# A two-block model on one core: x and c loaded first, eight products on GpSimd, and another order of attention steps and modulation pieces

## What is computed

```python
mod = c @ ada_w[l] + ada_b[l]                       # 6 x 1024 numbers: shifts, scales, gates
sh1, sc1, gt1, sh2, sc2, gt2 = split(mod, 6)
h = rmsnorm(x, norm1_g[l]) * (1.0 + sc1) + sh1
xr, yr, q, k, v, ga, gb = split(h @ w_in[l], 7)     # w_in: 1024 x 7168
xr = causal_dwconv(xr, conv_w[l], conv_b[l])
y_a = rg_lru(xr, ...) * gelu(yr)                    # a linear recurrence over the positions
q, k = head_rmsnorm(q, q_norm_g[l]), head_rmsnorm(k, k_norm_g[l])
y_b = stick_breaking_attention(q, k, v)             # 8 heads of 128
mix = sigmoid(ga) * y_a + sigmoid(gb) * y_b
x = x + gt1 * (mix @ w_out[l])
h2 = rmsnorm(x, norm2_g[l]) * (1.0 + sc2) + sh2
up = causal_dwconv(h2 @ ffn_up[l], ffn_conv_w[l], ffn_conv_b[l])
x = x + gt2 * ((gelu(up[:half]) * up[half:]) @ ffn_down[l])
```

## Time and profile before

| What | us |
|---|---|
| median of 3 runs | 1760.31 |
| lowest and highest | 1758.86 and 1767.95 |
| the profiled execution's own time | 1761.02 |
| its span | 1759.2 |
| TensorE busy | 1606.3 (91%) |
| VectorE busy | 620.0 (35%) |
| ScalarE busy | 351.0 (20%) |
| GpSimd busy | 0.2 (0%) |
| DMA, mean over the span | 310 GB/s |

### The profile page before, as it was taken

The page is one execution under the profiler, slowest core; times in us unless marked ns, Lnnn a source line. Parts: engine busy times, 40 slices in busy tenths (PEclk is TensorE's granted clock), DMA queues, the critical chain, the costliest instruction groups (busy, mean ns, idle before and its releaser), DMA issues. The chain is left out here.

```text
span 1759.2 us, 20527 instructions
## 1 busy us (share of the span) xinstructions
PE 1606.3 (91%) x7254; PEld 887.2 (50%) x7254; DVE 620.0 (35%) x1429; ACT 351.0 (20%) x647; POOL 0.2 (0%) x4
## 2 busy tenths in 40 slices
PE   1999899999999897879999988899999999999894
PEld 1888788788888674733333322233333333333222
DVE  5547762589720367232121111111112111221111
ACT  1124563332210124131111111101111111111102
POOL 0000000000000000000000000000000000000000
PEclk8999899999999998879999999999999999999998
DMA  9836673457863330229999999999999999999993
GB/s 399 343 126 245 266 284 132 153 224 295 366 255 127 124 131 1 96 86 380 416 416 416 415 417 416 417 416 417 416 417 400 383 383 416 416 417 415 417 415 127
DMA packets 93604, 545.46 MB, mean 310 GB/s; under 512 B 8944, under 2 KB 9456, under 8 KB 44304
## 3 DMA queue, kind: packets, MB, share of 16 engines
q1 hardware_dynamic: 92144, 540.74, 76.5%
q10 hardware_dynamic: 1312, 2.75, 0.4%
HBM read 542.41 MB, written 1.05 MB: 309 GB/s over the span
## 5 line engine op out<-in xcount | busy, mean ns | idle before, releaser
L898 PE MATMUL bank<-ring,scr 128*64 128x512 f32 x2048 | 456.5, 598 | 19.4 <-DMA ring<-in_w_mlp 19.2
L501 PE MATMUL bank<-hT,ring 128*128 128x256 f32 x1856 | 415.8, 385 | 24.5 <-ACT hT L1070 24.0
L501 PEld LDWEIGHTS bank<-hT,ring 128*128 128x128 f32 x1856 | 358.6, 194 | 79.6 <-issue 28.8
L898 PEld LDWEIGHTS bank<-ring,scr 128*64 128x64 f32 x2048 | 142.9, 137 | 314.5 <-issue 255.5
L931 PE MATMUL bank<-ring,hT 128*64 128x512 f32 x1024 | 234.1, 597 | 4.6 <-DMA ring<-in_w_mlp 3.5
L2090 DVE TENSOR_SCALAR scr<-bank 128x256 f32<-128x256 f32 x64 | 27.0, 422 | 396.4 <-PE bank L898 396.4
L931 PEld LDWEIGHTS bank<-ring,hT 128*64 128x64 f32 x1024 | 68.5, 136 | 143.6 <-issue 131.4
L2156 DVE COPY hT<-bank 64x512 f32<-64x512 f32 x32 | 22.2, 695 | 320.1 <-PE bank L931 290.2
L1359 ACT ACTIVATE scr<-scr 128x256 f32<-128x256 f32 x64 | 26.7, 417 | 503.8 <-DVE scr L2090 503.8
L1463 DVE SCALAR_TENSOR_TENSOR ring<-ring,cb 128x1024 f32<-128x1024 f32 x96 | 113.3, 1220 | 9.8 <-DMA cb<-in_cb 6.3
L646 PE MATMUL bank<-scr,ring 128*128 128x256 f32 x384 | 83.5, 379 | 1.6 <-ACT scr L1215 1.6
(11 more groups left out here) (365 smaller groups left out, 1288.4 us busy)
## 6 DMA issues: line engine op xcount, KB each, us to landing
ring<-in_w_mlp SPq DMA_DIRECT2D x384, 1024.0 KB, 20.1
ring<-in_w_in SPq DMA_DIRECT2D x28, 1024.0 KB, 20.4
ring<-in_ada_w SPq DMA_DIRECT2D x24, 1024.0 KB, 8.4
ring<-in_up SPq DMA_DIRECT2D x24, 1024.0 KB, 5.7
ring<-in_w_ada SPq DMA_DIRECT2D x24, 1024.0 KB, 7.5
ring<-in_down SPq DMA_DIRECT2D x12, 1024.0 KB, 13.9
ring<-in_w2in SPq DMA_DIRECT2D x6, 1024.0 KB, 9.5
ring<-in_w_out SPq DMA_DIRECT2D x4, 1024.0 KB, 8.0
```

The costliest lines, as they stand in the source:

```text
L501: ins = mm(b[:, 256 * j:256 * j + 256], v[:, k * 256 + j * 128:k * 256 + j * 128 + 128], rhs[:, k, :], start=(k == 0), stop=(k == 7))
L898: ins = mm(HID[0][n][64 * hf:64 * hf + 64, :], K.xe[0][x % 2][:, xo:xo + 64], v[:, o0:o0 + 512], start=False, stop=(k == 7), skip_group_ch ...
```

## The change

- `lay_pieces`: the modulation pieces (1, k) come two for each c instead of three pieces for each c; the pieces (2, 0) to (2, 4) lie between the ga chunks and (2, 5) to (2, 7) between the gb chunks.
- Start: SyncE issues `xT` and `cb` ahead of all ring pieces, ScalarE only `con` and then `col`. ScalarE loads the root's table at once, squares x and takes the root before it looks at `lam`. VectorE takes the reciprocal behind two modulation pieces instead of four; the eight products are made by GpSimd, in a new function `gpsimd_program`.
- Attention: step 7 moves behind the first ga chunk; steps 8, 9, 10 follow the next three; steps 11 and 12 the first two gb chunks. The gb chunks 2 and 3 are cut into halves of 8 matmuls, with steps 13, 14, 15 and 16 behind the four halves.
- VectorE uses two modulation pieces for each c, two in the first and one in each other ga stage, and one in each of the first three gb stages, and makes the parts of mix as soon as each can be made (`mixed`).

```diff
--- before.py
+++ after.py
@@ -287,13 +287,14 @@
             if c < 3:
                 w_in(("conv", c + 1), c + 1)
             plan.append((("rg", c), a["rg"][c], 512))
-            for i in range(3 * c, 3 * c + 3):
-                ada(1 + i // 8, [i % 8])
+            ada(1, [2 * c, 2 * c + 1])
         for c in range(4):
             w_in(("ga", c), 20 + c)
-            ada(2, [4 + c])
+            ada(2, [[0, 1], [2], [3], [4]][c])
         for c in range(4):
             w_in(("gb", c), 24 + c)
+            if c < 3:
+                ada(2, [5 + c])
         for c in range(4):
             plan.append((("w_out", c), a["w_out"][c], SLOT))
         for j in range(24):
@@ -418,6 +419,8 @@
 
     S, a = K.S, K.a
 
+    e.dma_start(K.xT[:, :, :], a["xT"]).then_inc(S.ld_x, 16)
+    e.dma_start(K.cb[:, :], a["cb"]).then_inc(S.ld_cb, 16)
     for i, (key, src, n) in enumerate(K.plan):
         if i >= RING:
             before = K.plan[i - RING][0]
@@ -588,7 +591,7 @@
         att_step(2 * c)
         if c < 3:
             chunk(("conv", c + 1))
-        att_step(2 * c + 1)
+            att_step(2 * c + 1)
         rg = landed(("rg", c))
         e.wait_ge(S.xc, c + 1)
         if c:
@@ -602,11 +605,20 @@
         ins.then_inc(S.piece_done, 1)
     for c in range(4):
         chunk(("ga", c))
-        att_step(8 + c)
-    for c in range(4):
-        chunk(("gb", c))
-        att_step(12 + c)
-    att_step(16)
+        att_step(7 + c)
+    for c in range(4):
+        if c < 2:
+            chunk(("gb", c))
+            att_step(11 + c)
+            continue
+        v, b = main(("gb", c))
+        for j in range(2):
+            for k in range(8):
+                ins = mm(b[:, 256 * j:256 * j + 256], v[:, k * 256 + j * 128:k * 256 + j * 128 + 128], K.hT[:, k, :],
+                         start=(k == 0), stop=(k == 7))
+            if j:
+                ins.then_inc(S.piece_done, 1)
+            att_step(9 + 2 * c + j)
 
 
     for c in range(4):
@@ -1071,19 +1083,18 @@
                 scale=K.mc[:, k:k + 1]).then_inc(S.h, 1)
 
 
-    e.dma_start(K.cb[:, :], a["cb"]).then_inc(S.ld_cb, 16)
+    e.dma_start(K.con[:, 0:256], a["consts"][:, 0:256]).then_inc(S.ld_col, 16)
     e.dma_start(K.col[:, :], a["cols"]).then_inc(S.ld_col, 16)
-    e.dma_start(K.con[:, 0:256], a["consts"][:, 0:256]).then_inc(S.ld_col, 16)
-    e.dma_start(K.xT[:, :, :], a["xT"]).then_inc(S.ld_x, 16)
+    e.wait_ge(S.consts, 3)
+    table(ACT.Sqrt)
+    e.wait_ge(S.ld_x, 16)
+    for c in range(4):
+        act(K.sq1[c], K.pair(K.xT, c), ACT.Square).then_inc(S.sq, 1)
+    norm_root(0, K.rst1)
     e.wait_ge(S.ld_col, 32)
     act(K.lt[0], K.C("lam", 0, 8), ACT.Abs).then_inc(S.act, done.one())
     e.wait_ge(S.act, done.n)
     act(K.lt[0], K.lt[0], ACT.Exp, scale=-1.0).then_inc(S.coef, 1)
-    e.wait_ge(S.ld_x, 16)
-    for c in range(4):
-        act(K.sq1[c], K.pair(K.xT, c), ACT.Square).then_inc(S.sq, 1)
-    e.wait_ge(S.consts, 3)
-    norm_root(0, K.rst1)
     modulate(0, 0)
 
 
@@ -1179,7 +1190,9 @@
             e.wait_ge(S.mixga, c - 1)
         act(K.Wt[2 + c % 2], K.main_bank(("ga", c))[:, :], ACT.Sigmoid).then_inc(S.ga, 1)
     for c in range(4):
-        att_step(12 + c)
+        att_step((11, 12, 13, 15)[c])
+        if c == 2:
+            att_step(14)
         landed(("gb", c))
         act(K.Wt[4 + c], K.main_bank(("gb", c))[:, :], ACT.Sigmoid).then_inc(S.gb, 1)
     e.wait_ge(S.ada_use, 24)
@@ -1474,13 +1487,10 @@
     e.memset(K.onec[:, 0:1], 1.0).then_inc(S.consts, 1)
     e.memset(K.halfpi[:, :], np.pi / 2).then_inc(S.consts, 1)
     e.wait_ge(S.ld_cb, 16)
-    for k in range(4):
+    for k in range(2):
         ada(0, k)
     norm_end(0, K.rst1)
-    e.wait_ge(S.rstd, 1)
-    for k in range(8):
-        tt_(K.hT[:, k, :], K.xT[:, k, :], K.rst1, ALU.mult).then_inc(S.hn, 1)
-    for k in range(4, 8):
+    for k in range(2, 8):
         ada(0, k)
     ada_bias(0, 0, 1)
     e.wait_ge(S.mod, 1)
@@ -1617,23 +1627,22 @@
         att_step(2 * c)
         if c < 3:
             conv(c + 1)
-        ada(1 + 3 * c // 8, 3 * c % 8)
-        att_step(2 * c + 1)
-        ada(1 + (3 * c + 1) // 8, (3 * c + 1) % 8)
+        ada(1, 2 * c)
+        if c < 3:
+            att_step(2 * c + 1)
+        ada(1, 2 * c + 1)
         recurrence(c)
-        ada(1 + (3 * c + 2) // 8, (3 * c + 2) % 8)
-    for c in range(4):
-        att_step(8 + c)
+    for c in range(4):
+        att_step(7 + c)
         mix = K.pair(K.mix, c)
         e.wait_ge(S.ga, c + 1)
         e.wait_ge(S.mixr, c + 1)
         tt_(mix, mix, K.Wt[2 + c % 2], ALU.mult).then_inc(S.mixga, 1)
-        ada(2, 4 + c)
-    ada_bias(0, 1, 3)
-    for c in range(4):
-        att_step(12 + c)
-    att_step(16)
-    for c in range(4):
+        if c == 0:
+            ada(2, 0)
+        ada(2, c + 1)
+
+    def mixed(c):
         mix, w = K.pair(K.mix, c), K.Wt[4 + c]
         e.wait_ge(S.gb, c + 1)
         e.wait_ge(S.att_y, 2 * c + 2)
@@ -1641,6 +1650,17 @@
         e.wait_ge(S.vec, done.n)
         e.wait_ge(S.mixga, c + 1)
         tt_(mix, mix, w, ALU.add).then_inc(S.mix, 1)
+
+    for c in range(3):
+        att_step(11 + c)
+        ada(2, 5 + c)
+        if c == 2:
+            att_step(14)
+        mixed(c)
+    ada_bias(0, 1, 3)
+    att_step(15)
+    att_step(16)
+    mixed(3)
 
 
     e.wait_ge(S.mod, 2)
@@ -2191,6 +2211,15 @@
         ins.then_inc(S.x, 1)
 
 
+def gpsimd_program(e, K):
+
+    S = K.S
+    e.wait_ge(S.ld_x, 16)
+    e.wait_ge(S.rstd, 1)
+    for k in range(8):
+        e.tensor_tensor(K.hT[:, k, :], K.xT[:, k, :], K.rst1, ALU.mult).then_inc(S.hn, 1)
+
+
 def program(nc, a, out):
     with ExitStack() as ctx:
         K = Board(nc, ctx, a, out)
@@ -2199,6 +2228,7 @@
         block.tensor(lambda e: tensor_program(e, K))
         block.scalar(lambda e: scalar_program(e, K))
         block.vector(lambda e: vector_program(e, K))
+        block.gpsimd(lambda e: gpsimd_program(e, K))
 
 
 def lay_out(i):
```

## The result

The changed kernel takes 1752.5 us (median of 10 runs, 1746.3 to 1758.9), the kernel before, run beside it, 1761.7 (median of 10, 1756.7 to 1770.2). The ratio is 0.994, with a 95% interval of 0.9919 to 0.9961: 7 to 14 us less.

What follows compares the result with a forecast made beforehand. TensorE was taken to bound the first block, reading the experts' weights the second half. Start 6.0 plus attention 1.1 gave 7.1 us: 1753.9 against the profiled execution, 1753.2 against the median; 8-in-10 range 1748.0 to 1759.0.

Steps and rivals of the forecast that it cites:

- What bounds, and that a gain passes on: Whole kernel: TensorE bounds the first block, weight reading the experts at 416 GB/s; first-block gains reach the end unchanged.
- Start without hindrance, 32.4: TensorE's first chunk: with no hold-up from GpSimd it starts at 32.4 instead of 42.35, a gain of 10.0 us.
- The products on GpSimd, eight times 0.50 us of hold-up: Start: each GpSimd product holds VectorE up 0.50 us, 4.0 in all; TensorE starts at 36.4, gain 6.0 us.
- Rival A: Start: GpSimd's products don't hold VectorE up; gain 11.1 us, 1749.2; chance 0.28.
- rival C: Start: GpSimd's products are long, 1.79 us each, and hold VectorE up; slower by 3.2, 1763.5; chance 0.06.
- Step 7: Attention, head 3: the 7.15 us wait at the sums goes, one of 6.9 comes at the output, with 3 of clock.
- Rival D: Attention: no new stall at head 3, because the recurrence of c = 3 is through earlier; 1743.3; chance 0.04.
- Halved chunks: End of attention: half chunks of 3.45 us leave waits of 1.9 us for head 6 and for head 7.
- No clock cost of the short waits: Attention, behind the two 1.9 us waits: nothing taken for lost clock, since each stands alone.
- Rival B: Attention: the short waits lower the clock, twice 1.7 us; gain 3.7, 1756.6; chance 0.12.
- w_out 14.0: The two w_out chunks take 14.0 us instead of 15.71, without the waits just ahead; 1.7 us back.
- The sum: Whole kernel: 6.0 us from the start plus 1.1 from the attention, 7.1 us gained, 1753.2 against the median.

Runs made afterwards that it cites:

- experiment 8: Changed kernel, but ScalarE and VectorE make step 7 ahead of the recurrence of c = 3 and steps 8 to 11 a stage earlier; 1745.1 us, ratio 0.9904.
- products late: Changed kernel, but VectorE makes the eight products behind the gains and GpSimd does nothing; 1749.5 us, ratio 0.9925.

## Why the prediction was right, and where it was off

- **What bounds, and that a gain passes on: right.** The stretch 900:1100 us moves 416 GB/s in every trace, TensorE's start and waits made the difference, and the FFN start and the medians go together over the kernels of the table. From a wait of TensorE ahead of the experts to its last one in the kernel it is 997.8 us before (754.42 to 1752.20) and 998.1 after (747.97 to 1746.06), but 1002.5 in the second trace of the changed kernel and 993 to 1003 over all traces here, so a single execution shows a gain of the first block only to within some 5 us.
- **Start without hindrance, 32.4: right.** 32.24 to 32.65 in the four kernels with late products whose pieces nothing lengthened. Two terms of it were off and made up for each other: the first piece came at 10.83, not 10.4, and the root was done at 14.67, not 15.6 (the sums took 5.75 us, not 6.8, their last rows at the higher clock), so the reciprocal started at 15.53 without the wait of 0.4 of the forecast. The landing of the first chunk's weights, forecast at 32.2, is what the start waits for in three of the four kernels (32.24 to 32.38).
- **The products on GpSimd, eight times 0.50 us of hold-up: right in kind, and 4.0 for what came to 4.2.** Chain end 35.2 forecast, 35.16 measured; TensorE 36.4 and 36.31. But the value was luck in part: a product is 0.69 us long by itself, not ScalarE's 0.50 that I took, and holds VectorE up for less than its length. Rival A (no hold-up) and rival C (1.79 us a product) fall. By the estimate from the figure of the Trainium skill (GPSIMD Engine Reference, section 3.1: 0.56 us a product, 4.5 us) TensorE would have started at 36.9, 0.6 late; the product alone measured 0.69, above that estimate.
- **Step 7: "the stall moves, and keeps its size": right.** 6.9 forecast at L569, 6.77 measured, no wait at the sums. The times on the way, worked out in the clock of before, are right too, once the 6.0 of the start are taken off: logits and weights done at 226.1 - 6.0 = 220.1 (L569 starts at 220.20). The clock behind the stall cost 2.0 us, not 3; behind the old one it was 3.1 (sums and gates from 209.99 to 215.27 where 2.6 are their time, and a chunk of 7.48 instead of 7.07). Rival D (the stall doesn't come) falls, though experiment 8 shows what it would have been worth.
- **Halved chunks: one term mis-sized.** Head 6 waited 1.94 (1.9 forecast), head 7 0.66, not 1.9. The step that failed is "a chunk of 6.9 covered that, half a chunk of 3.45 doesn't: 1.9 us of wait for head 6 and for head 7": it takes the 5.35 us from a head whose softplus starts with a table load. ScalarE in the changed kernel, head 6 and then head 7:

```profile
256.22 1.28 ACT L1126 ACT_TABLE_LOAD   x1
...
268.68 0.49 ACT L1124 ACTIVATE scr<-bank 128x384 f32<-128x384 f32 x1 [3.02 <-PE bank L553]
269.20 0.52 ACT L1126 ACTIVATE scr<-scr 128x384 f32<-128x384 f32 x1
```

  The weights of head 6 (L1133, an exponential) stand directly ahead of head 7 on ScalarE now, with no sigmoid between, so the table is there and 1.28 us fall away: 1.94 - 1.28 = 0.66. The order of ScalarE's steps, which the changed code shows, would have told it.
- **No clock cost of the short waits: wrong in part.** Rival B had 1.7 us for each of two; behind head 6 just that came, 1.7 us, in every trace of this order; behind head 7's 0.66 none. The reason given for taking nothing, that each wait stands alone, fails: head 6's wait stands alone too. That experiment 8's order has the same wait without the loss says that the length of the wait doesn't decide it; what does stays open.
- **w_out 14.0: right** (14.05), and no wait over 0.5 ahead of it (0.31).
- **The sum.** 7.1 forecast; 7.8 and 8.5 at the FFN start in two traces, 9.2 and 7.7 by the medians, 6.0 by the profiled span. In the first trace the waits gave 1.5 more than forecast (head 7 1.2 less, the 0.3 between the two heads not there, the stall itself 0.1 shorter, the wait ahead of w_out 0.1 longer), the clock behind the long stall 1.1 more; the clock behind head 6 took 1.7 and the first two chunks 0.2 (15.78 against 15.56 before): 7.1 + 1.5 + 1.1 - 1.7 - 0.2 = 7.8. So the forecast is near in part because two misses of opposite sign nearly cancel. The second trace has 0.7 more: its first chunk starts 0.15 earlier, its first two chunks take 15.43, and the chunk behind the stall 7.51. What the median of 9.2 shows beyond that is well inside its interval (7 to 14 us), and what the profiled span lacks is in the stages behind the FFN start.

## What to carry to other kernels

Before work is moved to an idle engine, ask what the two engines share, and what the work cost where it was: here eight products took 2.77 us of VectorE and then held it up for 4.2, while the same products a little later, where ScalarE follows them tile by tile, cost some 0.4 (TensorE at 32.65 in products late; the same chain without products would give 32.2, by the distances of the changed kernel). A stall that goes from one instruction of a chain leaves the chain as late as it was: look for the engine whose order makes the last input late (here the logits behind a recurrence), and change that order. Where chunks cover the steps of such a chain, count the steps against the chunks, and give each gap the cover it needs, not the same to all.

## What the runs showed that I had not expected

- GpSimd and VectorE in turns: beside VectorE's multiplications (two inputs in SBUF) a GpSimd product of 128x256 takes 1.65 us, alone 0.69, and adds 0.52 to the multiplication; a copy adds 0.18, a memset (0.26 us each) nothing.
- A wait of 1.94 us at the same step was followed by a clock at the lower level in seven of seven traces of one order, and in neither of two traces of another.
- Executions of the changed kernel lie 12.6 us apart (1746.3 to 1758.9), as much as its whole gain and more. Its two traces (spans 1753.2 and 1756.6) agree on the two chunks of the second block (15.70 and 15.66, 17.14 and 17.12); what makes the second the longer, though its FFN starts earlier, stands among the experts: from 747.97 to 1169.60 the first takes 421.6 us, the second, from 747.11 to 1173.98, 426.9, at a granted clock of 0.93 between 1100 and 1170 where the first has 1.00. Over all kernels here this stretch takes 417 to 427 us, and no edit touched it.
